# Two-layer trunk with top-2 experts on one core: in every work item the down product is issued ahead of the next item's gather

## The reference

```
h = rmsnorm(x, m_norm[layer])                          # (512, 1024)
group   = argmax over 4 of h @ w_group + b_group       # one group a token
experts = top 2 of the 8 experts of that group         # by h @ w_expert + b_expert
weight  = softmax weights, the two normalised to sum 1, times the group's probability
for each token t and each of its two experts e:
    hid = silu(h[t] @ w1[e]) * (h[t] @ w3[e])          # w1, w3: 1024 x 512
    x[t] += weight * (hid @ w2[e])                     # w2: 512 x 1024
```

## Time and profile before

| | |
|---|---|
| median of 3 runs | 1584.84 us (1584.27 to 1587.21) |
| the profiled execution: its time | 1583.66 us |
| the profiled execution: its span, first to last instruction | 1581.9 us |
| TensorE's matmuls busy | 1475.7 us, 93% of the span |
| VectorE busy | 982.9 us, 62% |
| ScalarE busy | 472.0 us, 30% |
| DMA | 461 MB, 291 GB/s over the span |
| mean granted TensorE clock | 0.981 of full speed |
| first *up* of layer 0's experts, and of layer 1's | 324.01 us and 1129.24 us |
| last *up* of layer 0's experts, and of layer 1's | 756.87 us and 1562.01 us |

### The profile page before, as it was taken

The page is one execution under the profiler, slowest core; times in us unless marked ns, Lnnn a source line. Parts: engine busy times, 40 slices in busy tenths (PEclk is TensorE's granted clock), DMA queues, the critical chain, the costliest instruction groups (busy, mean ns, idle before and its releaser), DMA issues.

```text
span 1581.9 us, 45769 instructions
## 1 busy us (share of the span) xinstructions
PE 1475.7 (93%) x18889; PEld 1001.3 (63%) x18890; DVE 982.9 (62%) x2116; ACT 472.0 (30%) x796; POOL 25.8 (2%) x64
## 2 busy tenths in 40 slices
PE   7999999999999899988999999989899998998977
PEld 6788888755555556555778875458655554554544
DVE  5346642377777677675744457853777676675656
ACT  6442221412222222221543354533222121221211
POOL 3000000000000000000000000000000000000000
PEclk9999999999999999999999999999999999998999
DMA  6321322989999999999521322126899999999996
GB/s 216 123 106 54 107 94 73 385 332 428 429 428 429 428 428 429 429 428 428 199 99 61 121 80 81 40 65 255 345 389 428 428 429 428 428 429 427 430 429 294
DMA packets 55482, 461.12 MB, mean 291 GB/s; under 512 B 4496, under 2 KB 4640, under 8 KB 30848
## 3 DMA queue, kind: packets, MB, share of 16 engines
q1 hardware_dynamic: 51728, 453.00, 69.1%
q10 hardware_dynamic: 2192, 4.23, 0.8%
q0 software_dynamic: 1504, 3.07, 0.7%
HBM read 458.15 MB, written 2.13 MB: 291 GB/s over the span
## 4 chain that ended last, share of the span: by engine, by line
PE 70%; DMA 24%; DVE 4%; issue 2%; SPq 0%; ACT 0%; DVEq 0%; ACTq 0%
DMA EB<-in_m_w 23%; PE ps L1472 15%; PE ps L1311 10%; PE ps L1313 10%; PE ps L1312 10%; PE ps L1461 6%; PE ps L1482 6%; PE ps L1444 4%; PE ps L1687 2%; PE ps L1722 1%; PE ps L1741 1%; PE ps L1756 1%; PE ps L1574 1%; PE ps L1307 1%; PE ps L1373 1%
## 5 line engine op out<-in xcount | busy, mean ns | idle before, releaser
L1472 PE MATMUL ps<-EB,SCR 128*32 128x256 f32 x6016 | 366.7, 399 | 67.5 <-DMA EB<-in_m_w 53.6
L1472 PEld LDWEIGHTS ps<-EB,SCR 128*32 128x32 f32 x6016 | 196.4, 115 | 230.0 <-issue 102.2
L989 DVE TENSOR_TENSOR X<-X,ps 128x1024 f32 x188 | 221.1, 1217 | 30.0 <-PE ps L1444 30.0
L1313 PE MATMUL ps<-EB_r 128*128 128x512 f32 x512 | 200.2, 391 | 0.0
L1461 PE MATMUL ps<-H,SCR 128*32 128x256 f32 x3072 | 185.7, 382 | 0.0
L1482 PE MATMUL ps<-EB,SCR 128*32 128x256 f32 x3008 | 179.7, 379 | 0.0
L664 ACT ACTIVATE SCR_r<-ps,SCR 128x256 f32 x94 | 44.5, 473 | 448.1 <-PE ps L1482 448.1
L980 DVE TENSOR_TENSOR SCR<-SCR,ps 128x128 f32<-128x128 f32 x94 | 36.9, 393 | 209.3 <-ACT SCR L661 209.3
L1482 PEld LDWEIGHTS ps<-EB,SCR 128*32 128x32 f32 x3008 | 97.8, 110 | 64.7
L1312 PE MATMUL ps<-EB_r 128*128 128x512 f32 x352 | 137.7, 391 | 0.0
L1461 PEld LDWEIGHTS ps<-H,SCR 128*32 128x32 f32 x3072 | 90.0, 109 | 62.2
(11 more groups left out here) (277 smaller groups left out, 1661.3 us busy)
## 6 DMA issues: line engine op xcount, KB each, us to landing
EB<-in_m_w SPq DMA_DIRECT2D x192, 2048.0 KB, 26.7
EB<-in_a_w_in SPq DMA_DIRECT2D x7, 2048.0 KB, 8.2
EB<-in_a_w_out SPq DMA_DIRECT2D x4, 2048.0 KB, 7.9
EB<-in_kv_w SPq DMA_DIRECT2D x4, 2048.0 KB, 13.6
EB<-in_b_w_qg SPq DMA_DIRECT2D x4, 2048.0 KB, 7.9
EB<-in_b_w_out SPq DMA_DIRECT2D x2, 2048.0 KB, 9.5
X<-in_x SPq DMA_DIRECT2D x4, 512.0 KB, 7.0
EB<-in_a_w_in SPq DMA_DIRECT2D x4, 512.0 KB, 9.8
```

The lines of the kernel that those rows point to most:

```text
L989: add = v.tensor_tensor(X_t, X_t, moved[1][:, :, t, :], ALU.add)
L1313: return mm(o, left[1], right[0], start=False, stop=stop)
L1472: last = mm(ps[0][g * CAP:(g + 1) * CAP, 0:2 * P].rearrange("p (w n) -> p w n", w=2), xT[:, k, :], w13_sb[s][:, :, k, g * P:(g + 1) * P], ...
```

## The change

In `expert` the call `gather(n + 1)` moves from ahead of the down product (and of its two waits) to behind it. Nothing else is edited; the down product's line is L1481 now.

```diff
@@ -1473,7 +1473,6 @@
                                           xT[:, k, :], w13_sb[s][:, :, k, g * P:(g + 1) * P], start=k == 0, stop=k == KD - 1)
                         last.then_inc(m["up"], 1)
                         move_items(n)
-                        gather(n + 1)
                         pe.wait_ge(m["hidT"], n + 1)
                         pe.wait_ge(m["w2"][s], 16 * loads)
 
@@ -1482,6 +1481,7 @@
                                 last = mm(ps[2][g * CAP:(g + 1) * CAP, CW:2 * CW], hidT[:, c, :],
                                           w2_sb[s][:, c, g * CW:(g + 1) * CW], start=c == 0, stop=c == KE - 1)
                         last.then_inc(m["down"], 1)
+                        gather(n + 1)
```

## The result

The changed kernel takes 1609.69 us in the median of four runs (1609.06 to 1610.19), beside 1584.55 for the kernel before on the same chip (four runs). The ratio is 1.0158, 95% interval 1.0145 to 1.017: 25 us slower. The forecast was 1614.6 us, within 1596 to 1634. The profiled execution took 1610.19 us, its span is 1608.4 us.

The account below looks back on a forecast made before the run. Bound by TensorE (70%) and partly by late weights (DMA 24%). 1.36 us over 88 middle items, 120 us, less 20 (rounds) and 71 (room), plus 2 (queue): +30.9 on 1583.66 gives 1614.6 us, range 1596 to 1634.

Parts of the forecast that it names:

- likeliest case: Whole kernel: the turn uncovered in every item, partly absorbed by time spent waiting for weights; 1614.6 us, chance 0.75.
- the room of the weights: TensorE's time in the experts that only late weights filled: 27 us on layer 0, 44 us on layer 1.
- Down's start: Each item: down waits for hidT and begins 0.16 us after it, at 408.04, with the gather at 409.79.
- The uncovered turn: Each item: gather, turn and xT are no longer covered by down; period 9.65 us against 8.29, +1.36 an item.
- The change of round: Between rounds of items: its loads run beside the turn, so its 1.14 us go, nine times a layer.
- The first rival: Changes of round still cost 1.14 us each, +10.3 on layer 0 and some +9 on layer 1; 1634 us, chance 0.10.
- the late piece: Layer 0, move at 364.97 in the old trace: 1.15 us behind its pattern, added again to the new sum.
- First and last item: Ends of each layer's experts: first period 10.76 us instead of 10.31, last 11.50 instead of 11.30.
- The slip at expert 4: Layer 1's weights queue: expert 4's w1, behind the third up, is issued 0.45 + 1.36 = 1.8 us later.
- The second, at expert 13: Layer 1's weights queue: expert 13's w1 waits for expert 10's third item, a slip of 2.9 us.
- the third rival: TensorE's clock falls, every up taking 5.35 instead of 3.66 us; 160 us on top, 1775 us, chance 0.05.
- the fourth rival: Layer end: down 1.6 us earlier gives back 1.6 us a layer; with the turn still covered 1580.4 us, chance 0.03.

Follow-up runs that it names:

- e1: Kernel before (old order) with only half of w1, w3 and w2 loaded from the fourth expert on; 1510.72 us, ratio 0.9537.
- e7: Kernel before with VectorE's four spread-matrix instructions for the layer's end moved from ahead of the loop to just ahead of the last item; 1583.74 us, ratio 0.9992.
- e4: Kernel before (old order) with the turn lengthened by three more gain multiplications into an unused tile; 1616.67 us, ratio 1.0205.
- e3: Changed kernel with the gather placed between two halves of the down product; 1588.56 us, ratio 1.0022 to the kernel before.
- e6: Changed kernel with the turn written straight into xT, the norm's gain multiplication left out; 1589.36 us, ratio 1.003 to the kernel before.
- e5: The change in layer 0's experts only, layer 1 in the old order; 1605.07 us, ratio 1.0128 to the kernel before.

## Why the prediction was right

Its likeliest case came true in its mechanisms: xT uncovered in every item, the change of a round hidden, the room of the weights used up on layer 0 and one wait left on layer 1. In size it was 4.5 us too high (+30.9 against +26.4 in the profiled execution). That it came this close is in part luck: on layer 1 a slip of the queue that was 2.2 us too large met a slower clock of 1.7 us that was left out.

- *Down's start.* Forecast 0.16 us behind hidT; measured 0.14. That is 0.08 more than from xT to *up*, where the wait sits on the matmul (0.06), and near the 0.16 of the memset's row. That the register instruction makes the difference is not shown by itself.
- *The uncovered turn.* Forecast 2.01 + 0.89 + 0.06 us from the gather's start to *up*; measured 1.98 + 0.96 = 2.94 (428.27 to 431.21). With the down product the period is 9.60 against the forecast 9.65. Over 45 items that is 2.2 us.
- *The change of round.* Forecast at nothing, measured at nothing: the timeline has 9.60 there, and the chain there is VectorE's, not "issue". e1 shows the same loads uncovered again, 19.7 us in 20 waits. The first rival did not come true.
- *The late piece of* move. I carried the 1.15 us of the earlier trace rows over; the changed kernel's trace shows no such piece there (363.99 to 373.60, 9.61 us). What makes it is open. It comes with the old order and all the weights: the two periods there are 8.42 and 9.50 us in the kernel before and 8.43 and 9.50 in e7, but 8.29 and 8.30 in e1, with the old order and half the weights.
- *First and last item.* Forecast 10.76 and 11.50, measured 10.57 and 11.38. The 10.76 doesn't follow from the forecast's own steps. Down at 329.90, the gather 1.75 later, then 2.01 + 0.89 + 0.06 give *up* at 334.61, 0.29 us later than before and not 0.45. The missing 0.16 is the hand-over from hidT, which isn't due in this item, as a row of the kernel before shows (timeline of VectorE):

```profile
328.90 0.31 DVE L983 STREAM_TRANSPOSE SCR<-SCR 128x128 f32<-128x128 f32 x1
```

  hidT was ready at 329.21, before *move* was through. Measured are 0.26 us (10.57 against 10.31).
- *Layer 0.* 10.57 + 45 x 9.60 + 11.38 = 453.95, as measured. Forecast 457.7. So the change is +21.1 and not +24.8: 2.2 us from the period, 1.15 from the late piece, 0.3 from the ends.
- *Layer 1.* One wait for weights was forecast, at expert 29, and it is the one in the trace, 2.7 us. The weights landed 405.85 us behind the first *up*, 2.45 us later than before, where I had 4.7. The slip at expert 4 is 1.6 us (issued 24.04 us behind the first *up* instead of 22.45) where 1.8 were forecast; the 0.16 of the first item is that difference. The second, at expert 13, was mis-sized: 0.9 us by the difference of the two, and not 2.9. Some 0.8 of the 2.0 us come from the items, by the forecast's own steps: w1 was issued 158.42 us behind the first *up* and not 159.43, and the queue was through 0.2 us earlier. The rest is the hand-over in the queue. I let the transfer begin 1.6 us behind its issue with the queue empty until then; here the queue was still draining when the issue came:

```profile
1306.00:1308.00 2.00, 2.00 (x44) 1.23 (x40) 1.93 (x6) 0.00 (x0) 0.00 (x0) 1.00 1.02 434
1308.00:1310.00 2.00, 2.00 (x52) 1.33 (x44) 0.77 (x3) 0.28 (x1) 0.00 (x0) 1.00 0.44 188
1310.00:1312.00 2.00, 1.90 (x42) 1.14 (x40) 1.71 (x3) 0.00 (x0) 0.00 (x0) 1.00 1.00 270
```

  That is the changed kernel's table by stretches around the issue at 1309.18 us (columns as in the earlier trace rows). The share of 2 us never falls under 0.44, where the earlier trace rows have 0.04. Against this stands something the sum left out: behind the 2.73 us of idle time the *up* ran at 1.2 GHz for a while, 5.35 us instead of 3.66, so the next period was 11.28. I had assumed full speed there, since the row with 2.59 us of idle time had it. Together +5.3 instead of +6.1.
- *The weights' queue gets weaker slices.* The table by stretches, layer 0 and layer 1, of the changed kernel:

```profile
345.00:745.00 400.00, 353.58 (x6688) 211.16 (x6684) 275.40 (x586) 83.66 (x124) 0.00 (x0) 1.00 0.97 408
1155.00:1535.00 380.00, 335.25 (x6336) 200.21 (x6336) 261.02 (x553) 81.02 (x119) 0.00 (x0) 1.00 0.99 419
```

  and of the kernel before:

```profile
345.00:745.00 400.00, 371.53 (x6996) 221.26 (x6992) 283.84 (x610) 87.73 (x130) 0.00 (x0) 0.98 1.00 425
1155.00:1535.00 380.00, 342.15 (x6288) 201.63 (x6284) 257.55 (x557) 81.08 (x119) 0.00 (x0) 0.96 1.01 429
```

  The DMA share falls from full to 0.97 on layer 0, and hardly on layer 1. The granted clock is the last number but two: 1.00 in both stretches after, 0.98 and 0.96 before. So the third rival went the other way: the changed kernel has the better clock.
- *The end.* Costed at nothing. Last *up* to the end of the span: 19.91 us before and 19.56 after. Down begins 1.66 us earlier in the last item (4.83 us behind *up*, not 6.49), and the end gained 0.35; the fourth rival had too little to give.

The clock rule that was weighed, of short idle spells that make the clock swing (the Trainium skill, TensorE: Matmul & The Clock Gate, "A second HAM failure mode: psum-queue depth-cycling"), did not show here: with 1.03 us of idle time in every 9.60, each plain *up* took 3.66 us at 2.4 GHz. e4 had 1.27 us in 9.67 and the same 3.66.

## What to carry to other kernels

Before moving a piece of work on the busiest engine, list what runs on other engines beside it. The gather and the down product cost TensorE the same in either order, but not the same to the engines behind it. The gather's result goes through a chain (turn, xT) before TensorE can go on, so it belongs first, and the down product, whose result is not needed so soon, runs while that chain does. Then ask how much of the time that a new order exposes is hidden by what bounds the kernel now: here the weights left 28 and 44.5 us a layer, so on layer 0 the first 0.44 us an item cost 2.5 us in all (e3) and 0.85 us cost 4.0 (e6), but the whole 1.31 cost 21.1.

## What the runs showed that was not expected

- *A clock that takes back what an earlier start gives.* e7's *up* began 1.11 us earlier and its successor only 0.07 us earlier, since TensorE got its full clock back 1 us later. Behind waits of 3.8 to 6.3 us for weights an *up* took between 4.93 and 6.57 us in all the runs, against 3.66 at full speed, so the gain of a kernel bound by such waits can vanish in the clock's timing.
- *No fixed length of idle time decides.* An *up* at full clock followed 2.59 us of idle time in the kernel before, 2.73 us in the changed one gave 5.35 us, and so did 2.32 us in e7. Yet e7 has full speed behind 2.81 us and e5 even behind 3.26:

```profile
653.45 3.66 PE L1472 MATMUL ps<-EB,SCR 128*32 128x256 f32 x64 [2.81 <-DMA EB<-in_m_w]
```

```profile
1465.96 3.66 PE L1472 MATMUL ps<-EB,SCR 128*32 128x256 f32 x64 [3.26 <-DMA EB<-in_m_w]
```

  (the first from e7's timeline of TensorE, the second from e5's).
- *Half the traffic, the same time.* On layer 0 the new order took 453.97 us with the full weights at 408 GB/s and 453.97 with half of them at 214. In this stretch the transfers beside the products slowed no item: the period is 9.60 us in both.
